# Tokens in column order behind the first output product, and neighbourhood attention over 512 keys a query

## What is computed

```
def neighborhood_attention(q, k, v, kc, vc, rpb):
    rows = s // GRID_W
    kr = min(NA_KR, rows)
...
    c_start = jnp.clip(col - NA_KC // 2, 0, GRID_W - NA_KC)
    c_idx = c_start[:, None] + jnp.arange(NA_KC)[None, :]
    c_off = c_idx - col[:, None] + (NA_KC - 1)
    scale = d ** -0.5

    def one_row(r):
        r_start = jnp.clip(r - kr // 2, 0, rows - kr)
        k_slab = lax.dynamic_slice_in_dim(kg, r_start, kr, axis=1)
        v_slab = lax.dynamic_slice_in_dim(vg, r_start, kr, axis=1)
...
```

## Time and profile before

| | |
|---|---|
| Median of 3 runs | 2091.49 us (2089.72 to 2093.75) |
| The profiled execution's own time | 2089.43 us |
| Its span, first to last instruction | 2087.6 us |
| PE, DVE, ACT, POOL busy | 88%, 29%, 23%, 14% of the span |
| Mean granted TensorE clock | 0.946 of full speed |

### The profile page before, as it was taken

The page is one execution under the profiler, slowest core; times in us unless marked ns, Lnnn a source line. Parts: engine busy times, 40 slices in busy tenths (PEclk is TensorE's granted clock), DMA queues, the critical chain, the costliest instruction groups (busy, mean ns, idle before and its releaser), DMA issues.

```text
span 2087.6 us, 21997 instructions
## 1 busy us (share of the span) xinstructions
PE 1828.3 (88%) x8958; PEld 1059.0 (51%) x8958; DVE 613.1 (29%) x1179; ACT 474.8 (23%) x969; POOL 292.6 (14%) x132
## 2 busy tenths in 40 slices
PE   7998998869897998979898888968999997668998
PEld 4796544553332434333242424328656895347876
DVE  3494763450200202020110202024465003431054
ACT  4243603330010100010000001022444223333231
POOL 2322833000000000000000000012100420004460
PEclk9998999989999999999999999995999997779999
DMA  6121356149999999999999999971200621002131
GB/s 230 57 90 72 82 189 181 41 182 405 421 420 421 420 423 424 425 421 420 421 421 420 424 423 425 421 306 41 81 1 1 111 81 41 0 1 91 41 121 41
DMA packets 97121, 482.20 MB, mean 231 GB/s; under 512 B 21572, under 2 KB 26020, under 8 KB 79648
## 3 DMA queue, kind: packets, MB, share of 16 engines
q1 hardware_dynamic: 96016, 478.84, 57.6%
q0 software_dynamic: 1040, 2.46, 0.8%
HBM read 477.22 MB, written 4.55 MB: 231 GB/s over the span
## 4 chain that ended last, share of the span: by engine, by line
PE 63%; DVE 12%; DMA 10%; SPq 5%; ACT 4%; issue 3%; POOL 1%; DVEq 0%; ACTq 0%; POOLq 0%
PE psum L504 23%; PE psum L1656 15%; DMA ring<-in_expert_w_down 9%; PE psum L1676 7%; SPq L1595 5%; PE psum L619 4%; PE psum L1639 3%; PE psum L653 3%; PE psum L1685 3%; PE psum L634 2%; PE psum L2221 2%; DVE work_area L982 1%; DVE small L725 1%; DVE work_area L1087 1%; PE psum L645 1%
## 5 line engine op out<-in xcount | busy, mean ns | idle before, releaser
L1656 PE MATMUL psum<-ring,work_area 128*64 128x512 f32 x2048 | 448.1, 594 | 35.8 <-DMA ring<-in_expert_w_gu 28.0
L1656 PEld LDWEIGHTS psum<-ring,work_area 128*64 128x64 f32 x2048 | 148.2, 137 | 329.1 <-issue 277.0
L1676 PE MATMUL psum<-ring,work_area 128*64 128x512 f32 x1024 | 234.9, 610 | 24.8 <-DMA ring<-in_expert_w_down 22.7
L1745 DVE TENSOR_TENSOR work_area<-psum,work_area 128x512 f32<-128x512 f32 x32 | 20.6, 686 | 596.6 <-ACT work_area L1708 596.6
L1676 PEld LDWEIGHTS psum<-ring,work_area 128*64 128x64 f32 x1024 | 74.5, 140 | 174.9 <-issue 147.2
L1842 POOL TENSOR_TENSOR hn<-x_res,ring 128x1024 f32<-128x1024 f32 x3 | 7.0, 2356 | 1039.3 <-DVE x_res L1752 1039.3
L1796 POOL TENSOR_TENSOR block_lo<-ring,part_hi 128x1024 fp32r<-128x1024 f32 x36 | 85.9, 2394 | 441.0 <-ACT part_hi L1789 441.0
L1708 ACT ACTIVATE work_area<-psum 128x512 f32<-128x512 f32 x32 | 17.4, 594 | 485.4 <-PE psum L1656 485.4
L504 PE MATMUL psum<-h_hi,part_hi 128*128 128x512 f32 x256 | 99.9, 390 | 1.0 <-DVE hn L765 1.0
L504 PE MATMUL psum<-h_lo,part_hi 128*128 128x512 f32 x256 | 99.7, 389 | 0.0
L504 PE MATMUL psum<-h_hi,block_lo 128*128 128x512 f32 x256 | 99.6, 389 | 0.0
(11 more groups left out here) (423 smaller groups left out, 2917.8 us busy)
## 6 DMA issues: line engine op xcount, KB each, us to landing
ring<-in_expert_w_gu SPq DMA_DIRECT2D x128, 2048.0 KB, 26.1
ring<-in_expert_w_down SPq DMA_DIRECT2D x64, 2048.0 KB, 21.7
ring<-in_w_in SPq DMA_DIRECT2D x12, 2048.0 KB, 7.8
ring<-in_w_mod SPq DMA_DIRECT2D x8, 1536.0 KB, 6.2
ring<-in_w_out SPq DMA_DIRECT2D x3, 2048.0 KB, 12.6
ring<-in_ca_wkv SPq DMA_DIRECT2D x1, 4096.0 KB, 16.5
work_area<-na_scratch SPq DMA_DIRECT2D x16, 224.0 KB, 5.7
ring<-in_w_in SPq DMA_DIRECT2D x3, 1024.0 KB, 18.4
```

Of the source, the lines that this page charges most:

```text
L1656: ins = pe.matmul(psum[h * 64:(h + 1) * 64, c, :], xsT[:, k, e * CAP:(e + 1) * CAP], w[:, (2 * c + h) * BANK:(2 * c + h + 1) * BANK], star ...
L1676: ins = pe.matmul(psum[n * 64:(n + 1) * 64, 6, :], hidT[b][:, j, h, :], w[:, j, n * BANK:(n + 1) * BANK], start=(q == 0 and j == 0), stop= ...
```

## The change

Three things change together.

First, the order of the tokens. From the first output product on, token (row r, column c) stands at place 8c + r instead of 64r + c, so that a tile of 128 tokens is 16 whole columns. The three producers of `ymixT` write in that order (`by_rows`, a view with a step of 8 elements), `x` is loaded a second time in that order, the routing reads and writes through the same view so that ties fall as before, the rope table of the second block is permuted, and the output is stored back through `in_tiles`.

Second, NA's keys. Queries are taken 8 columns further on (`SHIFT`, 64 tokens, with the first 64 repeated at the end of `qbT`), so that the windows of a query tile of 16 columns lie in just two tiles of keys. A unit then has 256 near keys and 256 context keys: 512 instead of 768. In the values' product each half of a query tile pair has its own two key tiles, so there are products over 128 columns. One reduction with a bias (zeros for the context) gives the negative maximum, one exponential the weights.

Third, the bias table. It is a `[q, e, h, 256]` table, e for the usual tiles and the one that wraps around. POOL turns `rpb` in DRAM element by element, spreads it with 16 DMAs, and SP loads it with 32 DMAs of 8 partitions each; DVE fills the rest.

```diff
-        const = sb("const_sb", C_COS + NTOK)
-        fill = sb("fill", 240)
+        const = sb("const_sb", C_END)
+        fill = sb("fill", 192)
...
-        pt_na = [cut(slot(5), 0, KT2, S), cut(slot(2), 0, KT2, S)]
-        p_na = [W[:, 0:NTOK], W[:, NTOK:2 * NTOK], slot(5)[:, 3072:3072 + NTOK], const[:, C_COS:C_COS + NTOK]]
+        na_table = W[:, na_at:na_zero].rearrange("p (e h c) -> p e h c", e=2, h=NA_H)
+        pt_na = [cut(slot(5), i * 2048, T, S) for i in range(2)]
+        p_na = [W[:, i * S:(i + 1) * S] for i in range(4)]
...
+        def by_rows(v, lo=0, hi=GRID_H):
+
+            return v.rearrange("p (w r) -> p r w", r=GRID_H)[:, lo:hi, :]
...
-                            act.activation(p[:, 0:segs[0]], p[:, 0:segs[0]], ACT.Exp, bias=neg_max(i),
-                                           accum_out=sums(i, 0)).then_inc(exp_biased, 1)
-                            act.activation(p[:, segs[0]:], score_at(i)[:, segs[0]:], ACT.Exp, bias=neg_max(i),
-                                           accum_out=sums(i, 1)).then_inc(exped, 1)
+                            act.activation(p, p, ACT.Exp, scale=-1.0, bias=neg_max(i), accum_out=sums(i)).then_inc(exped, 1)
...
-                            link(dve.tensor_tensor_reduce(
-                                out=pbuf[i % np_][:, 0:segs[0]], in0=score_at(i)[:, 0:segs[0]],
-                                in1=bias(heads[c][j], qt), scale=1.0, scalar=NEG * 2, op0=ALU.add, op1=ALU.max,
-                                accum_out=tmp_max(i)[:, 0:1]))
-                            link(dve.tensor_reduce(tmp_max(i)[:, 1:2], score_at(i)[:, segs[0]:], AX, ALU.max))
-                            dve.tensor_reduce(neg_max(i), tmp_max(i), AX, ALU.max, negate=True).then_inc(maxed, 1)
+                            v, kinds = bias(heads[c][j], qt)
+                            dve.tensor_tensor_reduce(
+                                out=kinds(pbuf[i % np_]), in0=kinds(score_at(i)), in1=v, scale=-1.0, scalar=-2 * NEG,
+                                op0=ALU.add, op1=ALU.min, accum_out=neg_max(i)).then_inc(maxed, 1)
...
-            affT = B.at(g)[0:N_EXP, :]
+            affT, left_rows = by_rows(B.at(g)[0:N_EXP, :]), rows_of(left)
...
-            dve.tensor_tensor(slotT, slotT, left, ALU.mult).then_inc(sem("slot_rows"), 1)
+            dve.tensor_tensor(by_rows(slots_by_col), rows_of(slotT), left_rows, ALU.mult).then_inc(sem("slot_rows"), 1)
...
+        def na_keys(h, qt):
+
+            keys = lambda t: kbT[odd(h), h // 2, t * P:(t + 1) * P]
+            at = lambda lo, hi: lambda score: score[:, lo:hi]
+            if qt < T - 1:
+                near = [(at(0, 2 * P), kbT[odd(h), h // 2, qt * P:(qt + 2) * P])]
+            else:
+                near = [(at(0, P), keys(qt)), (at(P, 2 * P), keys(0))]
+            return [(at(CTX, 2 * CTX), kbT[odd(h), h // 2, S:]), *near]
+
+        def na_values(h, qt):
+
+            v = lambda kt: vb[:, kt, h * HD:(h + 1) * HD]
+            return [(v(T), 2, 0, 2 * P), (v(T + 1), 3, 0, 2 * P), (v(qt), 0, 0, P), (v(qt + 1), 1, 0, P),
+                    (v(qt + 1), 0, P, 2 * P), (v((qt + 2) % T), 1, P, 2 * P)]
...
+            sp.wait_ge(hn_mix, T)
+            for t in range(T):
+                sp.dma_start(x_sb[:, t, :], in_tiles(a["x"][0])[t]).then_inc(sem("x_in0"), 16)
...
-            for i in range(2):
-                for h in range(NA_H):
-                    sp.dma_start(na_table[i * 64:(i + 1) * 64, h, :].rearrange("p (r c) -> p r c", r=14),
-                                 v[:, h, 1 - i:15 - i, :]).then_inc(sem("na_table_in"), 16)
+            for w in range(NA_KC):
+                first = NA_KC - 1 - w
+                for e, lo, n in ((0, 0, 2 * NA_KC), (1, w // 8 * NA_KC, NA_KC)):
+                    sp.dma_start(na_table[w * GRID_H:(w + 1) * GRID_H, e, :, lo * GRID_H:(lo + n) * GRID_H],
+                                 na_dram[e, :, :, first + lo:first + lo + n, :].rearrange("q h c r -> q h (c r)")
+                                 ).then_inc(sem("na_table_in"), 16)
```

More of the change, by code:

```diff
@@ L50 @@
 NEG = -1e30
+SHIFT = NA_KC // 2 * GRID_H
+QB = S + SHIFT
 SMALL = 680
@@ L556, in build, with attention @@
         at_recip = sm(8)
-        def attention(heads, segs, q_at, k_at, v_at, dv, pbuf, ptbuf, o_out, step=1, late=True, turners=(act, dve), bias=None,
-                      besides={}):
-            width, nseg = sum(segs), len(segs)
+        def attention(heads, width, q_at, k_at, v_at, dv, pbuf, ptbuf, o_out, step=1, late=True, turners=(act, dve), bias=None,
+                      turned_from=None, besides={}):
             nkt, np_ = width // P, len(pbuf)
@@ L571, in attention @@
             n_scores, per_turn = SCORE_BANKS // banks_each, nkt // banks_each
-            starts = [sum(segs[:i]) for i in range(nseg)]
             def score_at(u):
@@ L611, in scores_pe @@
             def scores_pe(first):
-                for s in range(nseg):
+                pieces = [k_at(heads[units[u][0]][units[u][2]], units[u][1]) for u in range(first, first + step)]
+                for s in range(len(pieces[0])):
                     for u in range(first, first + step):
@@ L618, in scores_pe @@
                             pe.wait_ge(exped, before + u - n_scores + 1)
-                        ins = pe.matmul(score_at(u)[:, starts[s]:starts[s] + segs[s]], q_at(heads[c][j], qt), k_at(heads[c][j], s),
-                                        start=True, stop=True)
-                        if s == nseg - 1:
+                        at, keys = pieces[u - first][s]
+                        ins = pe.matmul(at(score_at(u)), q_at(heads[c][j], qt), keys, start=True, stop=True)
+                        if s == len(pieces[0]) - 1:
                             ins.then_inc(scored, 1)
```

155 lines of the change are left out of this document (88 added, 67 removed).

## The result

The changed kernel takes 2036.71 us, the median of four runs (2028.09 to 2037.95), where the kernel before took 2092.26 us beside it. The ratio is 0.9727, with an interval of 0.9698 to 0.9756. It is faster, but 49 us slower than the 1988 us forecast, and outside the range. The profiled execution took 2037.95 us; its span is 2036.2 us, 51.4 less than before.

The account below looks back on a forecast made before the run. PE bounds the kernel, busy 88%; in NA it waits and runs slowly. NA falls from 161.1 to 58.8 us: 2089.43 - 102.3 + 0.5 (routing) = 1987.6, said as 1988 us; own range 1982 to 1995, wider 1980 to 2003.

Parts of the forecast that it names:

- POOL's table build: POOL's DMAs ahead of the experts: at 22 ns a run they take 9 us of mostly idle engines; nothing waits.
- The term set to nothing: POOL's preparation of the bias table in DRAM, ahead of the experts: adds nothing to the forecast time.
- Rival D: Ahead of the expert stream: single elements all pass one DMA engine and delay it; 2134 us at 60 ns each; 2%.
- The rule that was set aside: The eight turning DMAs: a plain transposing DMA is 19 times slower than the hardware's transpose; taken to change the sum by nothing.
- NA: Second block's attention stage: falls from 161.1 to 58.8 us, a gain of 102.3 us.
- The other bound: Values' products in NA: 128-column products cost half of 256-column ones, counting columns only; 2.5 us below the sum taken.
- The scores of two units: PE's scores in NA: 0.96 us in 12 of 16 steps, 1.07 in the other 4, together 15.8 us.
- the model: The first block's attention, 32 units and 512 keys, chain on PE: 6.48 us for four units, 59.64 us in all.
- The ends: NA's pipeline fill and drain: 5.3 us, plus 0.3 for a rounding of weights on ACT.
- Rivals A and B: In NA. A: waits stay in the open, anything above 2000 us, 10%. B: low clock stays, kernel 2041 us, 4%.
- Token order: Strided operations: nothing shows in the first attention; the routing costs 0 to 2.0 us more, 0.5 taken.
- Rival C: Routing: strides are dear by the 16-byte line rule, costing 2.0 us, kernel 1989 us; 30%, a variant of the forecast.

Follow-up runs that it names:

- build in mid-stream: The changed kernel with POOL's whole table preparation held back until half of the expert pairs are done: 2148.01 us, ratio 1.0261 to the kernel before.
- the one that turns in SBUF: The changed kernel with the biases loaded flat, turned by one POOL copy in SBUF and written out flat: 1990.73 us, ratio 0.9513 to the kernel before.
- flat rows: The changed kernel with each turning DMA copying its 465 floats as one contiguous run, biases in wrong places: 1989.51 us, ratio 0.951 to the kernel before.

## Why the prediction was wrong

**The step that failed** is the one on POOL's table build, and the number in it: "22 ns a run of one engine's time. At that rate the new ones take 9 us of engines that are idle for 72%", and "nothing waits for the table before NA". The last part is true, and no cover at all: what waited were the loads beside it. The term set to nothing was worth 46 to 47 us, the whole of the miss, since the four kernels without it and without a build in mid-stream take 1989.5 to 1991.5 us for a forecast of 1988. Three things were wrong in it:
- The price of the elements. The rate of 22 ns was that of runs of 64 bytes, and it was divided by sixteen as if the elements were shared out. Written as 31 by 15 they are not, on either queue. On POOL's, the record reads as if every engine went through all of them, and where they run nearly alone they take 41 us of all sixteen engines, not 5. On SyncE's they fit one engine, at 39 ns each. In elapsed time the whole is 128 us by SyncE, 186 us (50 ns an element) in the changed kernel, and 230 us (62 ns) in the full stream, where the forecast had 9.
- The neighbours. The forecast took the engines to be idle for 72% of the time and the elements to fit in there. But all sixteen are held by them at once, so the loads beside them slow down on every engine, at a busy share that stays near 1: 190 GB/s for 416 in mid-stream. From 466 to 516 us the changed kernel moved 105 GB/s and the one that turns in SBUF 348: 50 x (348 - 105) = 12.2 MB. With 3.5 MB from 430 to 466 (121 against 219) and 2.0 MB from 516 to 566 (379 against 419) the deficit is 17.7 MB, which at 420 GB/s is 42 of the 46 us. This is a second view of the loss, not an addition to the division by place.
- The engine that issues. POOL's issues of 3.6 us hold VectorE up for 3.4, 5.8 and 3.9 us at 336, 389 and 462 (4.13 for 0.75, 6.17 for 0.36, 4.09 for 0.17; the 6.67 of the L479 at 326.57 stands in every kernel, in the one before too). The forecast had POOL free and looked at POOL alone.

**Rival D** came nearest, "the single elements might all go through one DMA engine", and it was given 2% because "the turning DMAs have 465 elements each, which may be spread". That was never worked out from the shape of the DMA, 31 outside. D was right that the elements would not be shared out. In the changed kernel, though, it was not one engine that was held but nearly all sixteen. That the measured 186 us and 50 ns an element stand so near D's threshold of 178 us and 48 ns is in part luck, since they hold POOL's waits too. D's outcome was not right either: by its sum all of the gain would have gone, and 46 us did. It took the elements' time beyond the idle time as lost in full, while the loads go on at a part of their speed beside them, at 25% to 46% of it by the GB/s above. So there was a case in the middle, faster than before by less than forecast, that no rival held. With the build in mid-stream, which is another place than D's, a bad end like D's came too, 2148 us.

**The rule that was set aside.** The prediction named what the Trainium skill, VectorE: DVE Perf Modes, says under the three transpose paths of a plain DMA that transposes, and gave it no weight for 15 KB that nothing waits for. The size in bytes was the wrong thing to weigh. The page says this of a large step at the destination's innermost dimension, and the changed kernel's destination is written in order, so the rule fits these DMAs only loosely. And the turned order alone is not the evil: written as 15 by 31 the DMA transposes just as much, lands in 16.4 us for the 10.0 of flat rows (medians), and costs the kernel nothing that shows. No row here has the ratio of 19, since no run used the hardware's transpose.

**NA** was right as a mechanism and in size: 56.0 us for a forecast of 58.8. The terms: the values take 1.74 us for four units, not 2.05. The other bound, 1.73, was the right one: products of 128 columns cost half of those with 256 here, and the row of L655 that I preferred, 0.59 for its 8, is no model for them. That is 2.5 us. The scores of two units take 1.06 for the forecast 0.96, and 1.08 for 1.07 in the wrapped steps, which is 1.2 us the other way. Transposes (1.02) and spreading (0.59) were as in the model. The ends are 56.0 less PE's 52.0 by these terms (12 x 1.06, 4 x 1.08, 16 x 1.02, 8 x 0.59, 8 x 1.74), or 4.0 us for 5.6. Rivals A and B are out: no DVE or ACT on the steady chain, and a clock of 1.00.

**Token order** cost 0.39 us for the 0.5 taken. In the routing's part of the chain one operation changed, the product that writes the slots with a step, 0.69 to 1.08 us:

```profile
L1582 DVE TENSOR_TENSOR work_area<-work_area x1: 1066/1066/1066, 486.2 to 486.2; 16x512 f32<-16x512 f32 x1
```

From the first maximum to behind that product it is 15.02 us, 472.27 to 487.29, against 14.63 from 437.54 to 452.17. The strided readings of PSUM, the first maximum and the first replacement, cost nothing that shows: L1576 takes 0.70 in both. The rule on 16-byte lines in the Trainium skill, SBUF - State Buffer, agrees with this one store in kind, at a price of 0.39 us. On the DVE readings from PSUM, of which the rule does not speak, no penalty shows. Rival C's 2.0 us is out.

**What cost nothing**, as forecast: the second load of x (the kernel that turns in SBUF has it, and misses the forecast by 2.7 us in all), and the table's 32 loads on SP, 22 us of issue, with the projections ahead of NA at 111.69 us and the products behind it at 120.00. The expert loop is at 119.3 us a pair, except for its first pair. Behind NA the changed kernel is 2.9 us longer; about 2 of these stand in the kernels without the slow turning too (1987.5 - 1793.3 = 194.2 us for the one that turns in SBUF), and the clock there reads 0.95 and 0.96 for 0.97. The cause was not tried.

## What to carry to other kernels

Read a DMA's outermost dimension and its number of contiguous runs, not its bytes. Here 31 by 15 single elements cost 39 to 62 ns of elapsed time each and 15 by 31 cost 9 ns in the full stream, so try the order whose outer dimension can be divided among the engines, or turn small data by an operation in SBUF. Only these two orders were run. And "nothing waits for it" clears a transfer only of its own lateness: ask what must land while it is under way, and use GB/s, not the busy share, to see whether something is in its way.

## What the runs showed of the hardware that was not expected

- The DMA busy share reads the same, 0.98 to 1.03, whether the engines move 416, 190 or 105 GB/s. With almost only single elements from POOL's queue it is 0.91 at 6 GB/s, and with those from SyncE's queue 0.11 at 1 GB/s.
- On POOL's queue a DMA of 31 by 15 single elements shows sixteen sets of packets of 465 elements each, one of 15 by 31 sixteen packets of 31 elements. On SyncE's queue both show 465 elements in all.
- One issue of 465 elements takes SyncE 15 to 22 us and POOL 3.6 us with the 31 outside, and 0.85 and 0.78 us with the 15 outside (medians). With the 31 outside POOL also stands for 28 to 49 us after each two, once for 12 us after their last element (411 to 423).
- Single VectorE operations that take 0.2 to 0.8 us otherwise took 4 to 6 us in the changed kernel while POOL wrote two such long DMAs, whatever their size (2, 256 or 1,024 columns). They took their usual time when POOL's issues were short, or when SyncE issued.
- A write into SBUF with a step of 32 bytes, 512 elements on 16 partitions, cost 0.39 us more, and strided readings of PSUM cost nothing.
